# A shorter router, one more chunk in the projections, earlier decay sums and lighter mLSTM rounds in a two-layer block

## What is computed

```python
# layer 0: one projection, then 4 differential attention heads and 4 two-directional mLSTM heads
s = q @ k.T * 64**-0.5                       # per head two maps m = 0, 1
w = softmax(s[0]) - lam * softmax(s[1]);  o = rmsnorm(w @ v, subln_g)
b = cumsum(log_f)                            # decay sums, forward and backward in time
dmat = exp(b_t - b_s + log_i_s - m_t)        # masked; m_t is the row's maximum
sc = (mq @ mk.T) * dmat
h = (sc @ mv) / max(abs(sum(sc)), exp(-m_t)) # forward share plus backward share, times a gate
x = x + gate * (concat(o, h) @ w_out)
# layer 1 instead: real part of a 2-D DFT over positions and channels, then a linear map
# each layer: 16 experts in 4 groups of 4, router shared by the layers
aff = sigmoid(h @ router_w);  biased = aff + router_b
group = argmax over groups of the sum of the two largest of biased
e1, e2 = the two largest of biased in that group (the first of equals)
y = sum over e1, e2 of aff[e] / (aff[e1] + aff[e2]) * (silu(h @ w_gate[e]) * (h @ w_up[e])) @ w_down[e]
# shift, scale and gate of every norm come from ada_w (12 chunks of 512 columns a layer) and c
```

## Time and profile before

| | us |
|---|---|
| median of 3 runs | 921.25 |
| lowest, highest | 915.95, 924.74 |
| profiled execution | 915.92 |
| its span | 914.1 |
| TensorE busy | 770.0 (84%) |
| VectorE busy | 424.4 (46%) |
| ScalarE busy | 150.9 (17%) |

### The profile page before, as it was taken

One profiled execution on the slowest core, in us unless ns is written; L12 is line 12 of the kernel. 1 busy time (PEld: TensorE's weight loads), 2 busy tenths in 40 slices (PEclk: granted clock), 3 DMA queues, 4 the chain that ended last, 5 costly groups with the idle time before them and its releaser, 6 DMA issues.

```text
span 914.1 us, 19155 instructions
## 1 busy us (share of the span) xinstructions
PE 770.0 (84%) x7500; PEld 437.2 (48%) x7501; DVE 424.4 (46%) x1111; ACT 150.9 (17%) x332; POOL 32.7 (4%) x58
## 2 busy tenths in 40 slices
PE   8899999897987979995677986699889879597684
PEld 3544646344544435653345753374456437264342
DVE  3258899884897773321112342432643212122326
ACT  3311101313743021000000010240210001000001
POOL 0100000110000000000000001000000000000010
PEclk9699999998999999998879998999999979898878
DMA  9997997989201989969999899996569999999971
GB/s 336 360 369 264 373 352 273 326 299 396 70 1 33 392 307 371 416 245 419 420 422 422 369 401 418 395 415 264 195 249 420 413 419 420 422 421 421 419 316 47
DMA packets 81778, 303.75 MB, mean 332 GB/s; under 512 B 9072, under 2 KB 16288, under 8 KB 57072
## 3 DMA queue, kind: packets, MB, share of 16 engines
q1 hardware_dynamic: 67456, 282.49, 78.2%
q0 software_dynamic: 3552, 12.59, 3.6%
q10 hardware_dynamic: 10704, 7.75, 2.7%
HBM read 291.39 MB, written 14.68 MB: 335 GB/s over the span
## 4 chain that ended last, share of the span: by engine, by line
PE 51%; DMA 19%; DVE 17%; issue 5%; SPq 4%; ACT 3%; ACTq 0%; DVEq 0%
DMA raw<-in_w_up 17%; PE bank L1811 16%; PE bank L1825 7%; PE bank L1597 7%; PE bank L1792 4%; PE bank L1587 3%; PE bank L1740 3%; PE bank L2014 3%; DVE bias L908 2%; DMA consts_sb<-in_constants 2%; SPq L476 2%; SPq L457 1%; DVE arena L908 1%; DVE xl L1474 1%; DVE small L1081 1%
## 5 line engine op out<-in xcount | busy, mean ns | idle before, releaser
L1811 PE MATMUL bank<-raw,arena 128*32 128x256 f32 x3392 | 221.9, 414 | 69.5 <-DMA raw<-in_w_up 39.3
L1811 PEld LDWEIGHTS bank<-raw,arena 128*32 128x32 f32 x3392 | 128.4, 118 | 155.8 <-issue 108.3
L1362 DVE TENSOR_TENSOR arena<-arena,bank 128x128 f32<-128x128 f32 x53 | 15.3, 288 | 270.8 <-ACT arena L804 270.8
L1825 PE MATMUL bank<-raw,arena 128*32 128x256 f32 x1696 | 112.6, 400 | 14.9 <-issue 14.9
L1825 PEld LDWEIGHTS bank<-raw,arena 128*32 128x32 f32 x1696 | 64.6, 116 | 53.6 <-issue 26.7
L804 ACT ACTIVATE arena<-bank 128x128 f32<-128x128 f32 x53 | 14.7, 277 | 347.6 <-PE bank L1811 347.6
L1597 PE MATMUL bank<-ring,arena 128*128 128x512 f32 x160 | 71.4, 606 | 0.0
L1792 PE MATMUL bank<-arena 128*32 128x256 f32 x912 | 61.3, 381 | 8.4 <-DVE arena L1329 7.2
L908 DVE SCALAR_TENSOR_TENSOR bias<-ring,small,bias 128x512 f32<-128x512 f32 x77 | 57.9, 752 | 2.7
L1597 PEld LDWEIGHTS bank<-ring,arena 128*128 128x128 f32 x160 | 30.7, 194 | 38.4 <-issue 38.3
L908 DVE SCALAR_TENSOR_TENSOR arena<-ring,small,arena 128x512 f32<-128x512 f32 x63 | 47.4, 752 | 2.2
(11 more groups left out here) (269 smaller groups left out, 803.6 us busy)
## 6 DMA issues: line engine op xcount, KB each, us to landing
raw<-in_w_gate SPq DMA_DIRECT2D x64, 1024.0 KB, 19.6
raw<-in_w_up SPq DMA_DIRECT2D x64, 1024.0 KB, 21.7
raw<-in_w_down SPq DMA_DIRECT2D x64, 1024.0 KB, 21.7
ring<-in_ada_w SPq DMA_DIRECT2D x24, 2048.0 KB, 13.8
ring<-in_w_in SPq DMA_DIRECT2D x7, 2048.0 KB, 14.8
unit_results<-arena ACTq DMA_DIRECT2D x220, 32.0 KB, 5.8
ring<-in_w_out SPq DMA_DIRECT2D x2, 2048.0 KB, 23.3
ring<-in_w_fnet SPq DMA_DIRECT2D x2, 2048.0 KB, 17.4
```

The source lines that it names most:

```text
L1811: ins = mm(ps[4][j * S:(j + 1) * S, 0:2 * FW].rearrange("p (m n) -> p m n", m=2), xT[:, k, :], w[:, k % 4, :, j * FW:(j + 1) * FW], start= ...
L1825: ins = mm(ps[5][j * S:(j + 1) * S, 0:XW], hT_e[:, k, :], w[:, k % 2, j * XW:(j + 1) * XW], start=(k == 0), stop=(k == KF - 1))
```

## The change

- Chunk 20 is done behind item 21 (mv 3); chunks 21, 22 and 23 behind the attention, and none between norm and router.
- The decay sums run on TensorE between the last mv product and the o products, VectorE's part of them behind chunk 19. The first scores wait for the buffers of single items, not for all.
- A softmax output's square is taken seven rounds later, from the copy. In mLSTM rounds the shares are worked out ahead of the next maxima and ScalarE scales the forward weights.
- Router: the first tile is copied and its logits made while the second is normed; each tile's copy is half on ScalarE, half on VectorE; the logits are one product of 16 columns per 128 channels; the sigmoid's table is loaded ahead of the second copy. The experts are found by counting who beats whom in a group (`beats`, `rank`), with compares between the linked steps; the running sum over experts is one scan; slots are taken for both experts at once; three rank products in place of five; fillers: two fewer behind the logits, and fewer between the tiles. SP's pieces 12 and 13 wait for `lg_ps`.

```diff
-ADA_AFTER = {n: 4 + i for i, n in enumerate((0, 2, 4, 5, 6, 7, 8, 9, 11, 12, 14, 16, 17, 18, 19, 20))}
-FILL_AFTER = 4 + len(ADA_AFTER) - 1
+ADA_AFTER = {n: 4 + i for i, n in enumerate((0, 2, 4, 5, 6, 7, 8, 9, 11, 12, 14, 16, 17, 18, 19, 20, 21))}
+FILL_AFTER = 4 + len(ADA_AFTER) - 2
...
-                    sp.wait_ge(part_ps, l + 1)
+                    sp.wait_ge(lg_ps, l + 1)
...
-                    nc.scalar.activation(mg[:, t, h * HD:(h + 1) * HD], ps[7][:, 0:HD], ACT.Identity, scale=first)
-                    nc.scalar.activation(mx["xcst"][:, 224:352], ps[7][:, 0:HD], ACT.Square, scale=first,
-                                         accum_out=oss[:, it:it + 1]).then_inc(o_used, 1)
+                    nc.scalar.activation(mg[:, t, h * HD:(h + 1) * HD], ps[7][:, 0:HD], ACT.Identity, scale=first
+                                         ).then_inc(o_used, 1)
...
+            def o_square(it):
...
+                    act.wait_ge(o_used, it + 1)
+                    nc.scalar.activation(mx["xcst"][:, 224:352], mg[:, t, h * HD:(h + 1) * HD], ACT.Square,
+                                         accum_out=oss[:, it:it + 1]).then_inc(o_squared, 1)
+
+            def scale_forward(it):
...
+                    act.wait_ge(share_ready, it - 8 + 1)
+                    nc.scalar.activation(E_[:, o, :], E_[:, o, :], ACT.Identity, scale=att[:, 4 + o:5 + o]
+                                         ).then_inc(forward_scaled, 1)
...
             for it in range(16):
+                scale_forward(it)
                 if it + 1 < 16:
...
+                if it >= 7:
+                    o_square(it - 7)
...
+            def fT_copy(l, t):
+
+                act.wait_ge(ft_ps, 4 * l + 2 * t + 1)
+                nc.scalar.copy(fT[:, 0:4, t * P:(t + 1) * P], ps[4 + 2 * t][:].rearrange("p (k n) -> p k n", k=4)
+                               ).then_inc(ft_ready, 1)
...
+                    if k in (2, 4) and t:
+                        fT_copy(k // 2 - 1, 0)
...
                 nc.scalar.activation(s_done[:, 6 + l:7 + l], ident[:, 0:1], ACT.Sigmoid)
-                act.wait_ge(part_ps, l + 1)
-                nc.scalar.copy(lg_part, ps[5][:, 0:SEQ]).then_inc(part_ready, 1)
+                fT_copy(l, 1)
...
+                if (kind, a) == ("mv", 3):
+                    decay_parts()
                 ada_after(n)
-            dve.wait_ge(r_ps, 1)
...
-                    dve.wait_ge(prob, 2 * it + 2)
                     for m in range(2):
+                        dve.wait_ge(prob, 2 * it + 1 + m)
...
+            def shares(it):
+                o = 2 * (it % 2)
+                if it >= 8:
+                    dve.wait_ge(s_free, it - 8 + 1)
+                    dve.wait_ge(expm, it - 8 + 1)
+                    link(nc.vector.scalar_tensor_tensor(att[:, 4 + o:6 + o], att[:, 4 + o:6 + o], -1.0,
+                                                        att[:, 4 + o:6 + o], ALU.mult, ALU.max))
+                    link(nc.vector.tensor_tensor(att[:, 4 + o:6 + o], att[:, 4 + o:6 + o],
+                                                 att[:, 12 + o:14 + o], ALU.max))
+                    nc.vector.reciprocal(att[:, 4 + o:6 + o], att[:, 4 + o:6 + o]).then_inc(share_ready, 1)
...
-                    link(nc.vector.tensor_scalar(E_[:, o, :], E_[:, o, :], att[:, 4 + o:5 + o], None, ALU.mult))
+                    dve.wait_ge(share_ready, it - 8 + 1)
+                    dve.wait_ge(forward_scaled, it - 8 + 1)
                 nc.vector.scalar_tensor_tensor(E_[:, o, :], E_[:, o + 1, :], att[:, 5 + o:6 + o], E_[:, o, :],
                                                ALU.mult, ALU.add).then_inc(wc_ready, 1)
...
                 products(it)
+                shares(it)
                 if it + 1 < 16:
                     maxes(it + 1)
...
-            for c in ADA_LATE[:-1]:
+            for c in ADA_LATE:
                 ada0(c)
...
+            def fT_copy(l, t):
+
+                dve.wait_ge(ft_ps, 4 * l + 2 * t + 2)
+                nc.vector.tensor_copy(fT[:, 4:8, t * P:(t + 1) * P],
+                                      ps[5 + 2 * t][:].rearrange("p (k n) -> p k n", k=4)).then_inc(ft_half, 1)
...
+                fT_copy(l, 0)
                 norm(n, 1, scale, shift)
                 nc.vector.memset(ys, 0.0).then_inc(L[l]["y_ready"], 1)
+                fT_copy(l, 1)
...
+                def beaten(a):
+
+                    for lo, hi, op in ((0, a, ALU.is_ge), (a + 1, EG, ALU.is_gt)):
+                        if lo < hi:
+                            nc.vector.tensor_tensor(bt4[:, :, :, a, lo:hi], b4[:, :, :, lo:hi],
+                                                    b4[:, :, :, a:a + 1].to_broadcast([P, TT, NG, hi - lo]), op)
...
-                link(nc.vector.tensor_reduce(gs, pr, AX, ALU.max))
-                link(first_max(gs, g1, ing, 0, "first4", NG))
+                begun(nc.vector.tensor_reduce(gs, pr, AX, ALU.max))
+                beaten(0)
+                beaten(1)
+                done()
+                begun(nc.vector.tensor_reduce(s1[:, :, 0:1], gs, AX, ALU.max))
+                beaten(2)
+                beaten(3)
+                done()
...
+                begun(nc.vector.tensor_reduce(s1[:, :, 1:2], g1, AX, ALU.max))
+                nc.vector.reduce_sum(rank.rearrange("p t e -> p (t e)"),
+                                     beats.rearrange("p t (e b) -> p (t e) b", b=EG), axis=AX)
+                done()
...
+                def chosen_by(rank_is, number, t, dst):
+
+                    return nc.vector.scalar_tensor_tensor(
+                        dst.rearrange("p (a g) -> p a g", g=NG), rank[:, t, :].rearrange("p (g a) -> p a g", g=NG),
+                        float(number), ing[:, t:t + 1, :].to_broadcast([P, EG, NG]), rank_is, ALU.mult)
+
+                for t in range(TT):
+                    ins = chosen_by(ALU.is_lt, 2, t, t16[:, t, :])
+                ins.then_inc(route_m, 1)
...
-                src, dst = runA, runB
-                for step in (1, 2, 4, 8):
-                    link(nc.vector.tensor_tensor(dst[:, NE:2 * NE], src[:, NE:2 * NE],
-                                                 src[:, NE - step:2 * NE - step], ALU.add))
-                    src, dst = dst, src
...
+                nc.vector.tensor_copy(cnt_i[:], counts).then_inc(count_ready, 1)
+                done()
+                link(nc.vector.reduce_sum(runA, some, axis=AX))
+                link(nc.vector.tensor_tensor_scan(runB[:, 1:NE + 1], ones[:, 0:NE], runA, 0.0, ALU.mult, ALU.add))
...
+                of_both(slots)
+                link(nc.vector.reduce_sum(slot_f.rearrange("p t q -> p (t q)"),
+                                          picked.rearrange("p t (q e) -> p (t q) e", q=2), axis=AX))
+                link(nc.vector.tensor_tensor(
+                    Pq, bc(cst("iota"), TT * 2, 2 * S), slot_f.rearrange("p t (q a) -> p (t q) a", a=1).to_broadcast(
+                        [P, TT * 2, 2 * S]), ALU.is_equal))
...
             dve.wait_ge(mod_ready, 6)
             mix_in(0, mod0[:, 0, :], mod0[:, 2, :], mod0[:, 1, :], None, (gain_in, 32))
-            ada0(2 * N_ADA - 1)
             route(0)
...
+            def decay_sums():
+
+                pe.wait_ge(lf_ready, 1)
...
+                if (kind, a) == ("o", 1):
+                    pe.wait_ge(b_ready, 1)
...
+                if (kind, a) == ("mv", 3):
+                    decay_sums()
...
-            pe.wait_ge(b_ready, 1)
...
+            pe.wait_ge(evac_a, EV_A[ITEMS.index(("mv", 1))])
             scores(0)
+            pe.wait_ge(evac_a, EV_A[ITEMS.index(("o", 0))])
             scores(1)
+            pe.wait_ge(evac_a, N_EV_A)
...
-                            for c in range(10, 12):
-                                sum_mod0(c, c - 10)
-                        keep_busy(3 + 2 * l, 7)
...
-                for q in range(2):
-                    for j in range(4):
-                        ins = mm(ps[5][32 * j:32 * j + 32, 0:SEQ], rw_s[:, 2 * j + q, :], fT[:, 2 * j + q, :],
-                                 start=(q == 0), stop=(q == 1))
...
-                keep_busy(5, 4)
...
+                def logits(t):
+
+                    for k in range(KD):
+                        if k == 0:
+                            pe.wait_ge(ft_ready, 2 * l + t + 1)
+                        if k == 4:
+                            pe.wait_ge(ft_half, 2 * l + t + 1)
+                        ins = mm(ps[4][:, t * NE:(t + 1) * NE], fT[:, k, t * P:(t + 1) * P], rw_s[:, k, 0:NE],
+                                 start=(k == 0), stop=(k == KD - 1))
+                    return ins
+
+                if l == 0:
+                    pe.wait_ge(mod_ready, 6)
+                turn_f(0)
+                if l == 0:
+                    for c in range(10, 12):
+                        sum_mod0(c, c - 10)
+                else:
+                    keep_busy(2, 7)
+                logits(0)
+                keep_busy(1, 7)
+                turn_f(1)
```

(9 more changed lines are left out.)

199 lines of the change are left out of this document (88 added, 111 removed).

## The result

The changed kernel took 892.79 us in the median (889.69 to 894.47, four runs); the ratio to the runs of before beside it is 0.9694, 95% interval 0.9626 to 0.9761. Its profiled execution took 889.69 us (span 887.9), 26.2 less than the one of before. A fourth run of the kernel before took 2631.89 us and counts in no comparison. Forecast were 898.0 us (889 to 911), and 23.2 less. Both profiles happen to be at the short end of their kernel: over all comparisons the kernel before has a median of 917.7 us in 47 runs and the changed one, run again, of 894.4 in ten. That difference is **23.3 us**.

A forecast was written before the change was run, and what follows sets the result against it. No single engine bounds the kernel; stages do, and time saved ahead of the first expert counts in full. Savings of 3.9 + 1.5 + 3.1 + 9.6 + 5.1 = 23.2 us from the 921.25 us median gave 898.0 us, range 889 to 911.

The forecast's parts named there:

- Bound by stages, not swallowed by the weights: Whole kernel: no single engine decides; time taken out ahead of the first expert moves everything behind it.
- the forecast's own signs of being wrong: VectorE idle before the combine, TensorE waiting for weights, fillers of 0.9 us, or layer 0 ending less early than its gather.
- Term 1: Decay sums ahead of the o projection: hand-off and cold scores go, first maximum at 214.4 us; saves 3.9 us.
- Term 2: Chunk 20 into projections, chunk 23 ahead of the mix: nothing moves under the output projection; VectorE's 1.70 us idle covers chunk 23's wait.
- Term 3: Eight softmax rounds: the square leaves ScalarE's round; saves 1.5 us, bounds nothing and 2.8.
- Term 4: mLSTM rounds: the forward weights' scale goes to ScalarE; net 0.45 us in each of seven rounds, saves 3.1 us.
- Term 5: Layer 0's router: shorter path and warm fillers, gather at 335.8 instead of 345.42 us; saves 9.6 us.
- Term 6: Layer 1's router: the same savings without a chunk or cold fillers; saves 5.1 us.
- The rival of the clock: Routers: TensorE's clock stays low, losing 3.3 us in layer 0 and 3.2 in layer 1; 904.5 us; chance 12%.
- ScalarE's hand-off: Attention rounds: it takes the scale's place, so Term 3 and Term 4 go; saving 18.6, 902.6 us; chance 9%.
- the slower case: Clock goes low in the logits and stays low in layer 0's units behind them; up to 947 us; chance 4%.
- The weights: Weight transfers set the end, so only 2 MB (5 us) taken ahead is won; 916 us; chance 7%.

The follow-up runs named there:

- experiment 7: Changed kernel with eight more filler matmuls on TensorE ahead of layer 0's gather: 902.85 us, ratio 0.9829.
- experiment 1: Changed kernel with the decay sums and VectorE's decay parts put back behind the o projection: 896.51 us, ratio 0.9745.
- experiment 8: Changed kernel with chunk 20 back behind the attention, so four chunks stand there: 899.50 us, ratio 0.978.
- experiment 3: Changed kernel with the scale of the mLSTM rounds' forward weights back on VectorE: 899.79 us, ratio 0.9795.
- experiment 10: Changed kernel with the old selection, running sum and `weigh` on VectorE, chunk 23 and logits as changed: 904.51 us, ratio 0.9878.
- experiment 2: Changed kernel with chunk 23 alone put back between norm and router of layer 0: 898.55 us, ratio 0.9761.
- experiment 6: Changed kernel without any filler matmuls in either router: 901.86 us, ratio 0.9829.
- experiment 5: Changed kernel with each of the selection's 13 pair sums and compares waiting for the one before, same instruction count: 897.75 us, ratio 0.9798.

## Why the prediction was right, step by step

- **Bound by stages, not swallowed by the weights.** Held; experiment 7 shows it from the other side. But the place has less room than I said: 4 to 5 us of gap were forecast for the first eight units, and at a share of 0.96 there are 2.0. One of the forecast's own signs of being wrong did come, since layer 0 ended less early (20.4 us) than its gather began (22.0). It cannot be told from scatter: the stretch between takes 306.0 to 308.6 us in the profiles where nothing was edited there, and took 306.97 before.
- **Term 1** (3.9; the 214.4 us beside it give 4.0): 4.25 in experiment 1, and probably 0.5 more in the stage behind. Hand-off and cold scores as written.
- **Term 2** (nothing): held in the sum, not in its cover. Chunk 23 waited 2.23 us, not under 1.70; the third residual came 0.6 later against the projection's start, and the fourth, which waits for TensorE, at the same 28.09. Without the move, experiment 8 loses 8.0.
- **Term 3** (1.5, bounds 0 and 2.8): the mis-sized one, 0.7. I took the middle between bounds; the row that decided it, TensorE's 0.42 us wait, stands only twice in the stage, and VectorE gets 0.34 of each. The other 0.5 us of the stage came from four score passes of 2.08 us before and 1.13 after; experiment 1 has the 2.08 again, so they go with term 1.
- **Term 4** (3.1): 3.6 in experiment 3, 3.9 in the table. A round fell by 0.54, not 0.45: that is the scale's 0.52 and a little more, so the 0.07 written for the products' end was not paid.
- **Term 5** (9.6): 10.0, of which 9.9 from the second transposes on. By the rows shown, with what was written: the selection starts 3.4 us earlier against these transposes (3.3) and takes 2.8 less (2.8), VectorE has the ranks 1.1 sooner (1.1), the slots take 1.3 less (1.3), and the fillers outlast VectorE by 0.1 instead of 1.4 (0.3). The experiments agree: 4.4 for selection and slots, 0.35 of it slow ranks (experiment 10), and 4.3 for chunk 23's place (experiment 2).
- **Term 6** (5.1): 5.4.
- **The rival of the clock** (12%) is not dead: it came true in three of ten layer-0 routers, at up to 2.6 us, not in layer 1. The mistake was to treat it as a property of the kernel; it is one of each execution. *ScalarE's hand-off* fell with experiment 3, *the slower case* with every profile: the clock is 1.00 in the 52 us behind the gather, and 0.96 behind a router without fillers (experiment 6). *The weights* fell too: TensorE waits for none in the first eight units. Its longest wait there is for VectorE, 1.27 us as before (1.28).
- **The Trainium skill** (VectorE: DVE Perf Modes, The DRAIN you can't avoid) would have made the two routers together 2.8 us dearer; in experiment 5 it is the waits that cost 1.53 us in one router at the same count. The page's next section, Two Vector instructions with no wait between them, has instructions that are not held back start before the earlier ones have finished. That one agrees with the rows (six sums in 0.56 us); I should have weighed it too.
- **The first comparison's 28.5 us** (921.25 to 892.79) were no larger effect: 2.6 us of the profiles' 26.2 lie ahead of the first edit, and the pooled medians give 23.3.
- **Luck in the number.** That 23.2 and 23.3 agree to 0.1 us is luck: the five edited stages of the table gave 24.8 us together, and the median of the kernel before alone moves from 916.7 to 921.0 us between chips. The forecast of 898.0 us was 5.2 too high, mainly because it started from a median of three runs that lay 3.5 us above the 917.7 of 47.

## What to carry to other kernels

Cut both traces at the same events before explaining a difference: a stage that repeats to hundredths tells more than a median over runs that scatter by 1%. When small VectorE steps set the path, count the waits as well as the instructions: a step with a wait took 0.21 us here, one without 0.09. And look for idle times of two to three microseconds on TensorE ahead of work that it bounds: fillers of a size that just fits cost nothing in the profile and were worth 5.4 us between two medians, about half of which the filled places explain.
